# Query heads interleaved so that they turn four at a time, and a new table of places for the mixers of a two-layer decoder step

## The reference, cut to what matters

```python
qa, ka, va, iq, ik, iw, za, qb, kb, vb, zb = _split(h @ w_in, AB_SIZES)   # qa: 8 heads of 64
...
# mixer A, per block of 128 query rows
sc = jnp.where(vis, index_scores(iqb, ik, iwb), -jnp.inf)     # relu(iq . ik) weighted over 4 heads
_, sel = lax.top_k(sc, topk)                                  # 256 keys of each row
return sparse_attend(qb, gather_rows(k, sel), gather_rows(v, sel), ok)   # 8 query, 2 key/value heads
...
# mixer B: retention, 4 heads, a state carried from chunk to chunk
obn = (obf - mu) * lax.rsqrt(var + EPS) * gn_gain
ya = oa.reshape(Bn, T, A_WIDTH) * jax.nn.silu(za)
yb = (obn.reshape(Bn, T, B_WIDTH) * jax.nn.silu(zb)).astype(za.dtype)
return jnp.concatenate([ya, yb], axis=-1) @ w_out
```

## Time and profile before

| | |
|---|---|
| median of 3 runs | 3401.28 us (3400.18 to 3405.79) |
| profiled execution | 3402.73 us, its span 3401.2 us |
| busy over the span | TensorE 3131.7 us (92%), VectorE 1827.7 (54%), ScalarE 1437.2 (42%), GpSimd 833.3 (24%) |
| 300 to 1690 us, the mixers | TensorE 1253.0 of 1390.0 us, VectorE 989.4, ScalarE 805.0 |

### The profile page before, as it was taken

One profiled execution on the slowest core, in us unless ns is written; L12 is line 12 of the kernel. 1 busy time (PEld: TensorE's weight loads), 2 busy tenths in 40 slices (PEclk: granted clock), 3 DMA queues, 4 the chain that ended last, 5 costly groups with the idle time before them and its releaser, 6 DMA issues. The chain is left out here.

```text
span 3401.2 us, 47063 instructions
## 1 busy us (share of the span) xinstructions
PE 3131.7 (92%) x15557; PEld 1711.8 (50%) x15557; DVE 1827.7 (54%) x3850; ACT 1437.2 (42%) x2966; POOL 833.3 (24%) x1596
## 2 busy tenths in 40 slices
PE   8998989999998989978877999999999979999998
PEld 4554444444444444444544445444445446667665
DVE  0000497678877888884331341441431667776774
ACT  2221114666676767777422111112111236655652
POOL 2332234322222212100000000000000157674671
PEclk9999999999999999999978999999999989998999
DMA  6567676555443433310077111111011143225321
GB/s 196 181 186 238 207 231 210 181 161 167 149 135 119 125 112 104 106 61 29 26 254 258 64 47 68 40 59 70 27 53 51 43 135 107 86 96 153 112 76 69
DMA packets 260396, 407.36 MB, mean 120 GB/s; under 512 B 47896, under 2 KB 131137, under 8 KB 258977
## 3 DMA queue, kind: packets, MB, share of 16 engines
q1 hardware_dynamic: 237156, 387.51, 35.4%
q0 software_dynamic: 4096, 8.40, 0.9%
q10 hardware_dynamic: 18912, 8.53, 0.9%
HBM read 324.25 MB, written 103.03 MB: 126 GB/s over the span
## 5 line engine op out<-in xcount | busy, mean ns | idle before, releaser
L2585 PE MATMUL QB<-hT,w_c 128*128 128x512 f32 x1024 | 449.3, 593 | 0.0
L814 PE MATMUL PB<-wb,hT_ahead 128*128 128x512 f32 x832 | 419.3, 631 | 10.2 <-PEq L4191 5.0
L2585 PEld LDWEIGHTS QB<-hT,w_c 128*128 128x128 f32 x1024 | 190.3, 190 | 217.5 <-issue 217.4
L358 PE MATMUL P0A<-w_all,hT 128*128 128x512 f32 (+1 forms) x816 | 268.2, 489 | 2.5 <-issue 2.5
L1007 ACT COPY ptT<-PT 128x512 f32<-128x512 f32 (+3 forms) x320 | 163.8, 518 | 248.5 <-PE PT L825 248.1
L2436 PE MATMUL QA<-arena,hT 128*128 128x512 f32 (+1 forms) x768 | 255.1, 488 | 5.8 <-issue 3.0
L3639 PE MATMUL RPJ<-w_co,oT 128*128 128x512 f32 x544 | 244.4, 598 | 1.8 <-DVE y L3942 1.0
L963 ACT ACTIVATE signs_out<-isc,mid 128x512 bf16<-128x512 f32 (+6 forms) x168 | 229.5, 1366 | 26.6 <-DVE mid L1107 25.5
L1119 DVE TENSOR_SCALAR_CACHE_REDUCE band<-isc,mid 128x384 bf16<-128x384 f32 (+6 forms) x168 | 236.4, 1407 | 1.3
L814 PEld LDWEIGHTS PB<-wb,hT_ahead 128*128 128x128 f32 x832 | 150.0, 199 | 170.0 <-issue 155.0
L802 PE MATMUL PS<-kT,qT 64*128 64x512 f32 (+3 forms) x544 | 155.5, 596 | 59.2 <-DVE mxc L1167 58.8
(11 more groups left out here) (543 smaller groups left out, 5320.5 us busy)
## 6 DMA issues: line engine op xcount, KB each, us to landing
wb<-in_w_in_ab SPq DMA_DIRECT2D x272, 512.0 KB, 3.8
out_c_all<-crow SPq DMA_DIRECT2D x256, 64.0 KB, 1.7
pra<-out_pr_all SPq DMA_DIRECT2D x16, 546.0 KB, 4.7
x_rows<-in_x_all SPq DMA_DIRECT2D x17, 512.0 KB, 5.5
out_hT_all<-hT SPq DMA_DIRECT2D x17, 512.0 KB, 3.0
arena<-out_c_all SPq DMA_DIRECT2D x17, 512.0 KB, 4.6
arena<-out_gc_rows SPq DMA_DIRECT2D x17, 512.0 KB, 4.3
cv<-out_c_all SPq DMA_DIRECT2D x17, 512.0 KB, 5.4
```

Source lines behind the costliest of these rows:

```text
L358: ins = pe.matmul(PA[u % 6][:, 0:b - a], hT[:, t % 3, c, :], w_all[:, c, a:b], start=(c == 0), stop=(c == KD - 1))
L814: ins = pe.matmul(b_bank(g, n)[:, :], h_of(g)[:, 2 * q + k, :], wb[:, u % 4, k, :], start=(q == 0 and k == 0), stop=(q == 3 and k == 1))
L2585: ins = pe.matmul(PB[b % 2][:, 0:N], w_c[:, c, b * P:(b + 1) * P], hT[:, c, 0:N], start=(c == 0), stop=(c == KD - 1))
```

## The change

Two edits. First, the host puts the query columns of the input projection into the order (0, 4, 1, 5, 2, 6, 3, 7) of heads, so that heads h and h + 4 stand side by side; `turn_q` then turns 128 columns at once, four transposes in place of eight half ones. Where sample rows are turned, the addresses follow; the count of instructions there is the same. Second, nearly all kinds of step get another place. No step is added or dropped, and no wait is.

```diff
-            add(b + 10, "pe", "turn_q", f)
-            add(b + 11, "pe", "turn_k", f)
+            add(b + 2, "pe", "turn_q", f)
+            add(b + 9, "pe", "turn_k", f)
...
-            add(b + 17, "pool", "qdecay", f)
+            add(b + 32, "pool", "qdecay", f)
...
-                    add(p, "pe", "index", f, c, j)
-                    add(p + 2, "act", "relu", f, c, j)
+                    add(p - 2, "pe", "index", f, c, j)
+                    add(p + 1, "act", "relu", f, c, j)
...
-                        add(p + 0.3, "act", "copy_p", t, r, a, c)
-                    add(p + 1.2 * d + 0.4, "pe", "times_v", t, r, c)
+                        add(p + 3.3, "act", "copy_p", t, r, a, c)
+                    add(p + 1.2 * d + 2.4, "pe", "times_v", t, r, c)
...
-            add(b + 103, "dve", "out_a", t)
+            add(b + 110, "dve", "out_a", t)
...
-        add(place + 3.2, "act", "move", s, k)
+        add(place + 1.7, "act", "move", s, k)
...
-                for h in range(AH):
-                    a, r = divmod(h, 4)
-                    ins = turn_half(pe, PX[0][a * HD:(a + 1) * HD, r * P:(r + 1) * P],
-                                    pra[:, h * HD:(h + 1) * HD], ident[:, :], a)
+                for r in range(4):
+                    ins = pe.transpose(PX[0][:, r * P:(r + 1) * P], pra[:, C_QA + r * P:C_QA + (r + 1) * P], ident[:, :])
...
-        "w_in_ab": inp["w_in_ab"][0], "norm_w": inp["norm_w"], "gn_ret": inp["gn_ret"],
+        "w_in_ab": np.concatenate([inp["w_in_ab"][0][:, 0:AH * HD].reshape(D, 2, AH // 2, HD).transpose(0, 2, 1, 3).reshape(D, -1),
+                                   inp["w_in_ab"][0][:, AH * HD:]], 1), "norm_w": inp["norm_w"], "gn_ret": inp["gn_ret"],
```

More of the change, by code:

```diff
@@ L417, in mixers_order @@
             add(b + 10, "pool", "kdecay", f)
-            add(b + 10, "pe", "turn_q", f)
-            add(b + 11, "pe", "turn_k", f)
+            add(b + 2, "pe", "turn_q", f)
+            add(b + 9, "pe", "turn_k", f)
             add(b + 12, "act", "copy_q", f)
-            add(b + 12.5, "pe", "turn_b", f)
-            add(b + 13, "act", "copy_k", f)
+            add(b + 13, "pe", "turn_b", f)
+            add(b + 13.5, "act", "copy_k", f)
             add(b + 14, "act", "copy_b", f)
-            add(b + 16, "act", "tanh", f)
-            add(b + 17, "pool", "qdecay", f)
+            add(b + 14, "act", "tanh", f)
+            add(b + 32, "pool", "qdecay", f)
             add(b + 18, "pe", "ret_scores", f)
             add(b + 18.5, "pe", "ret_state", f)
-            add(b + 20, "dve", "ret_mask", f)
-            add(b + 22, "dve", "gates", f)
+            add(b + 21, "dve", "ret_mask", f)
+            add(b + 24, "dve", "gates", f)
             add(b + 23, "pe", "ret_out", f)
             add(b + 25, "dve", "ret_update", f)
-            add(b + 25.5, "act", "ret_copy", f)
+            add(b + 23.5, "act", "ret_copy", f)
             add(b + 29, "dve", "gn_mean", f)
-            add(b + 31, "pool", "gn_centre", f)
-            add(b + 37, "dve", "gn_square", f)
+            add(b + 33, "pool", "gn_centre", f)
+            add(b + 41.5, "dve", "gn_square", f)
             add(b + 39, "pool", "gn_gate", f)
@@ L441, in mixers_order @@
                     p = b + 30 + 50.0 * k / len(units)
-                    add(p, "pe", "index", f, c, j)
-                    add(p + 2, "act", "relu", f, c, j)
+                    add(p - 2, "pe", "index", f, c, j)
+                    add(p + 1, "act", "relu", f, c, j)
                     add(p + 4, "dve", "weigh", f, c, j)
-                add(b + 88, "dve", "bounds", f)
+                add(b + 89, "dve", "bounds", f)
         g = n + 4
@@ L450, in mixers_order @@
             for k in range(16):
-                add(b + 8 + 5.5 * k, "pe", "project", g, k // 4, k % 4)
+                add(b + 8 + 5.5 * k + 1, "pe", "project", g, k // 4, k % 4)
                 if g or k >= 4:
@@ L454, in mixers_order @@
             for k in range(4):
-                add(b + 8 + 5.5 * (4 * k + 3) + 1, "act", "keep_b", g, k)
+                add(b + 8 + 5.5 * (4 * k + 3) + 4, "act", "keep_b", g, k)
         if g == NT:
@@ L470, in mixers_order @@
         elif 0 <= s < 2:
-            add(b + 76, "pool", "causal", s)
+            add(b + 68, "pool", "causal", s)
         t = n
@@ L477, in mixers_order @@
                 for c in range(k):
-                    add(q + 20.0 * c / k, "pe", "scores", t, r, c)
+                    add(q + 20.0 * c / k + 1, "pe", "scores", t, r, c)
                     add(q + 20.0 * (c + 0.7) / k, "dve", "masked", t, r, c)
                 add(q + 20, "dve", "maxima", t, r)
-                add(q + 21, "act", "exp", t, r)
+                add(q + 21.5, "act", "exp", t, r)
                 d = 8.0 / k
@@ L486, in mixers_order @@
                         add(p, "pe", "turn_p", t, r, a, c)
-                        add(p + 0.3, "act", "copy_p", t, r, a, c)
-                    add(p + 1.2 * d + 0.4, "pe", "times_v", t, r, c)
-            add(b + 84, "dve", "inverse", t)
+                        add(p + 3.3, "act", "copy_p", t, r, a, c)
+                    add(p + 1.2 * d + 2.4, "pe", "times_v", t, r, c)
+            add(b + 86, "dve", "inverse", t)
             add(b + 86, "pool", "gate_a", t)
-            add(b + 101.5, "act", "copy_o", t)
-            add(b + 102.2, "pe", "turn_o", t)
-            add(b + 103, "dve", "out_a", t)
+            add(b + 103.5, "act", "copy_o", t)
+            add(b + 107.2, "pe", "turn_o", t)
+            add(b + 110, "dve", "out_a", t)
             add(b + 104, "sp", "store_ya", t)
@@ L1829, in _ @@
             pe.wait_ge(S["rope4"], after(1))
-            for n, base in enumerate((C_QA, C_QA + 256)):
+            for n in range(2):
                 for r in range(4):
                     for a in range(2):
-                        c0 = n * P + r * SR
-                        ins = turn_half(pe, PO[0][a * HD:(a + 1) * HD, c0:c0 + SR],
-                                        pr[:, base + r * HD:base + (r + 1) * HD], ident[0:SR, 0:SR], a)
+                        c0, q0 = n * P + r * SR, C_QA + (2 * r + n) * HD
+                        ins = turn_half(pe, PO[0][a * HD:(a + 1) * HD, c0:c0 + SR], pr[:, q0:q0 + HD], ident[0:SR, 0:SR], a)
             ins.then_inc(S["q4_ps"], 1)
```

8 lines of the change are left out of this document (4 added, 4 removed).

## The result

The changed kernel takes **3307.87 us** (median of 4 runs, 3307.19 to 3308.76), beside 3400.73 us before (4 runs); the ratio is **0.9727**, 95% interval 0.9715 to 0.9739. The direction was right, the size wrong by a factor of three.

The account below looks back on a forecast made before the run. TensorE, busiest throughout the mixers, was taken as the bound, with gains in its pauses and clock. 15.3 + 2.6 + 4.2 + 4.7 + 4.0 + 9 - 14 + 5 = 30.8 us saved gave 3370 us, range 3342 to 3402.

Parts of the forecast that it names:

- the term for the copies of transposed tiles: TensorE's 17.8 us of pauses for copies, with `times_v` later: half saved, 9 us, bounds 0 and 17.8.
- a risk alone (3442 us): Slower rival: `copy_p` later on ScalarE delays transposes, half a microsecond in each of 144 pairs, 72 us; chance 0.12.
- A microsecond of TensorE's work counts nearly everywhere: Premise for all three mixer stretches: TensorE is busiest, so gains lie in its work, pauses and clock.
- The solid chain of VectorE: VectorE's unbroken steps from 1053.53 to 1073.79 us before round 9's `masked`; of them only `out_a` (0.60 us) leaves.
- Turning the query heads: Four transposes replace twelve records of `turn_q`: 1.02 us saved in each of 15 blocks, 15.3 us.
- `turn_q` ahead of the second `scores`: In rounds 8 to 12 `turn_q` fills part of TensorE's boundary pause: 2.6 us more saved.
- Boundary chain: VectorE at seven boundaries into rounds 7 to 13: `out_a` leaving saves 4.2 us, `relu` 0.67 us earlier saves 4.7.
- Output turn: In eight rounds `turn_q` ahead of `turn_o` covers TensorE's wait for the copy just issued: 4.0 us saved.
- Exponentials: Longer TensorE waits for `exp` in rounds 8 to 15: 14 us lost, bounds 0 (ScalarE reaching `exp` earlier) and 21.
- Clock: Shorter boundary pauses return a quarter of the 21.5 us of full clock not granted in rounds 7 to 12: 5 us.
- All other places: `qdecay`, `gates`, `gn_square`, `tanh`, `keep_b`, `bounds`, `copy_o`: put at nothing, as steps of engines with time to spare.

Follow-up runs that it names:

- e8_copy_p_old: The changed kernel with `copy_p` alone back at its old place on ScalarE (+0.3 instead of +3.3), `times_v` still late: 3348.68 us, ratio 0.984.
- e10_times_v_old: The changed kernel with `times_v` alone back at its old place (+0.4 instead of +2.4), `copy_p` still late: 3322.69 us, ratio 0.9769.
- e7: The kernel before with four turns, and copies, output, boundary, index, `relu` and other turn steps at new places, the rest old: 3331.53 us, ratio 0.9794.
- e11: The changed kernel with projection, `keep_b`, scores, `exp` and `move` back at their old places: 3316.64 us, ratio 0.9743.
- e15_relu_old: The changed kernel with `relu` alone back at its old place (+2 instead of +1), `index` still early: 3318.07 us, ratio 0.9739.

## Why the prediction was wrong

**The step that failed** is the term for the copies of transposed tiles. I sized it by TensorE's pauses there (9 us, bounds 0 and 17.8), which assumes that a place on ScalarE costs only where TensorE itself waits. `times_v` is worth 15 us, close to the upper bound. But `copy_p`'s move on ScalarE I had counted as a risk alone (3442 us), and it is worth 41: it took VectorE's waits for `relu` from 78.9 to 37.0, and TensorE's pauses for `masked`, `exp`, `keep_b` and `relu` from 85.7 to 51.7. What led to it stands one part earlier in the forecast. "A microsecond of TensorE's work counts nearly everywhere" came from its busy share, 90.6% in rounds 7 to 12; I then read VectorE's last pause before the boundary (2.38 us) and not the sum of all its pauses for `relu`, 114.8 us. The solid chain of VectorE, which I took as the bound on what the boundaries could give back, held: the pauses that open rounds 9 to 12 are 24.2 us before and 19.0 after, 5.2 less. The gain lay elsewhere in the rounds, which I had not counted. Over which steps the shorter waits for `relu` become time there is traced only in part, by the pauses in `e8_copy_p_old`.

Over the kernel before, the changed one and 17 variants of them, the time goes with these waits: a straight line through them has a slope of 1.10 us of time for each us of relu waits (correlation 0.97), no kernel further than 16 us from it. That is a relation and no proof: the sum of all pauses of TensorE fits nearly as well (correlation 0.96, slope 1.6). What shows the cause is the single edits above, in which one place on ScalarE or TensorE moved both. Below 38 us the relation ends.

The Trainium skill (Perfetto Trace Analysis, Identifying the Most-Contended Engine) advises to take the engine with the highest occupancy and optimize it first, with the caution that TensorE's busy share is a poor measure of its headroom. This case fits the caution: taking work off the engine that is busy 92% of the span gave 8 us, and a new order of the queues, with no engine's work changed, gave about 90 (0.9728). The Trainium skill (Perfetto Trace Analysis, Optimization Strategy) tells to follow what blocks a gap of that engine back to its source. Here that leads from TensorE over VectorE's `masked` to the `relu` of ScalarE, and to the copy ahead of it only if one asks next what ScalarE stood for.

By the steps of the prediction:

- *Turning the query heads*, 15.3 us: the records fell from twelve to four, as said, but alone they gave 8 us (0.9977), and on top of the new order 4.6 us, which is inside the noise (0.9728 and 0.9727). The size was wrong by half. `masked` rose by 5.2 us and the lower clock lasted 31 us longer in the mixers (127 and 96 us); which of the two took how much of the rest stays open.
- *`turn_q` ahead of the second `scores`*, 2.6 us: it runs ahead of the pause, as drawn (1010.96). Not tested apart.
- *Boundary chain*, 8.9 us: at round 9 right, 8.07 to 6.00 where 6.3 was forecast. But the total fell by 31.5 us and not by 12, most of it ahead of round 9 and 7.7 of it into the wait for `o_copy`. `relu` earlier by 0.67 us was the smallest part of what came to VectorE, and the earlier `index` had no term at all, where the pair is worth 26 us.
- *Output turn*, 4.0 us: nothing. The waits for `oT_a` are 6.2 us in 9, to the digit. Early in the mixers `turn_q` stands ahead of the last `times_v`, and the copy can't start before that product; a step fills a pause only if it stands between the product and the turn. `e10_times_v_old` shows it: with `times_v` back ahead of `turn_q`, that wait is 0.7 us, once.
- *Exponentials*, -14 us: the waits went from 25.6 to 22.7. The long pause that I had drawn is there (the longest is 4.5 us, as worked out), but there are 17 and not 26: ScalarE, which no longer stands at copies, reaches `exp` sooner. I had named this as the lower bound and taken the other end.
- *Clock*, 5 us: rounds 7 to 12 went from 0.96 to 0.97, as said. Over the whole mixers the lower clock lasted 96 us before and 80 us after, which at half speed is 8 us of work; here the mechanism and about the size were right.
- *All other places*, nothing: together with the projection, scores, `exp`, `move` and the output projection they are worth 24 us, the last step from `e7` to the full change. Some 9 of them come back with `e11`, and how the rest divides was not tested.

The experiments put in their place, from the turns up: copies and output steps 40, index group 24, the rest 24, turns 8; and the parts don't add freely, `copy_p` being worth 10 us alone and 41 in the full order.

## What to carry to other kernels

Where several engines run in-order queues that meet at semaphores, read the list of waits of every engine, and not of the busiest alone: ask of each long sum what stands in the queue behind the waiting step, and who waits for that. In this kernel a copy that merely waited for its data cost nothing itself (from +2.3 to +3.3 ScalarE's pauses at it fell by 14 us and no time was won), but what stood ready behind it did. So put such a step behind those whose data is there, and the producer of its data earlier, until the buffer that it holds is wanted. The curve had a flat bottom here, between two and three places. Try moves in sets too, and not only one at a time: with `copy_p` late alone, ScalarE stood at `relu` instead.

## What the runs showed of the hardware

A transpose of 128 columns has a median record of 273 ns (the 64 of `turn_o` in the mixers), but in a row they start 0.11 us apart. The timeline of TensorE after, at `turn_k` in an early round:

```profile
587.05 0.27 PE L687 MATMUL PX<-ident,pra 128*128 128x128 f32 x1
587.16 0.27 PE L688 MATMUL PX<-ident,pra 128*128 128x128 f32 x1
587.27 0.27 PE L689 MATMUL PX<-ident,pra 128*128 128x128 f32 x1
```

In round 9, behind the pause of 6.00 us, the same three start 0.26 and 0.22 us apart (1020.98, 1021.24, 1021.46), with records of 0.47 and 0.42 us. The granted clock is 0.50 over 1018.4 to 1024.0 us, the lower level of 1.2 GHz, and 1.00 over 585 to 590.

The busy time of TensorE depends on how often it pauses, by the order alone 34.9 us with the same 6509 records. More than half of that is not the clock but the last record ahead of each pause, which counts in full up to its modelled end: 0.35 us on average (41.3 us in 117), where a transpose in a row adds only 0.11. That is how the profile counts, and no work done.

The time of one and the same kernel goes with the clock that it was granted. The four runs of `e15_relu_old` took 3308.6 us at a mean clock of 0.969, 3314.9 at 0.967, and 3321.2 and 3321.3 at 0.964. What lowered it in the longer runs is not shown, but a difference of a few us between two kernels says little unless their clocks are compared.
